# Two-layer hybrid encoder on one core: another order between layer 0's mixer and its experts, row turns ahead of the third modulation tile, and q products that take hT chunk by chunk

## The chip, the core and the metric

One core of one Trainium2 chip runs the whole kernel in one launch. Five engines matter: TensorE (PE in the rows, PEld its weight loads), VectorE (DVE), ScalarE (ACT), GpSimd (POOL) and SyncE (SP), which only issues DMAs here. Each takes its instructions in the order in which they are written and waits at semaphores; nothing is scheduled by a compiler. The metric is the device time of one execution in microseconds, 942.29 for the kernel before (median of three).

## The reference, cut to what matters

256 tokens of width 1024 go through two layers, all in float32. The part that the change touches:

```
mod = silu(c) @ ada_w[layer] + ada_b[layer]            # six rows of 1024: shift, scale, gate, twice
h = rmsnorm(x) * norm_mix_g * (1 + scale) + shift
z = h @ w_in                                           # q 512, k and v 256, xr 512, gate 512
m = concat([window_attention(q, k, v), rg_lru(xr) * gelu(gate)]) @ w_out      # layer 0's mixer
x = x + g_m * m
h = rmsnorm(x) * norm_ffn_g * (1 + scale_f) + shift_f
group = argmax(h @ wg + bg); two best of the group's 4 experts by h @ we + be
x = x + g_f * sum over experts of gate_e * (silu(h @ w1[e]) * (h @ w3[e])) @ w2[e]
```

Layer 1 has an S5 state-space mixer in place of attention and LRU (`y = C h + d u`, with complex tables made from `s5_b`, `s5_c` and the poles), a GLU, and again 16 experts in 4 groups. A final norm ends the kernel.

## The kernel before, in words

All state lives in SBUF. `x` is [128, 2, 1024]: two blocks of 128 tokens. `hT` is the normalised, modulated input turned to features by tokens, in 8 chunks of 128 features; TensorE turns `xhat` (`turn_x`), ScalarE writes chunks 0, 1, 4, 5 and VectorE 2, 3, 6, 7 (`modulate`, semaphores `hT_act` and `hT_dve`). Weights come in tiles of 2 MB: `ring` has six slots, and one more place, `aslot` in `work`, serves the modulation weights. SyncE issues these DMAs in one fixed order; before each it waits until the last reader of the slot has signalled.

**Front.** The first four modulation tiles (`ada(0, 4)`: eight products each, condition column by weights into one row of `bank[7]`) give layer 0's first shift and scale. TensorE turns small parameter rows to columns (`tr` of `rows` and `brow`, ScalarE copies them at L635 and L636), ScalarE copies the modulation row (`rows_out`, L642), `ada_cols` makes columns of it, VectorE adds the bias, and then both engines modulate. The q products (L1429) wait for all of `hT`. GpSimd issues small loads beside this, among them four for the LRU's block-diagonal gate weights (`gaw`), which are used at about 102 us.

**Mixer's exit.** The output product has four tiles (`mix_out`, L1563), token block b by column half h, each in two halves of the inner dimension: attention's first, LRU's second. Between the second halves stand `ada_cols(1)` (twelve more modulation rows to columns, L1387) and `gate_row(0)` (L1412), which spreads the gate g_m over all partitions; ScalarE copies it to `grow` (L629, L630). VectorE's `residual` then multiplies and adds tile by tile (L1109, L1110) and signals `x_new`.

**Tables of layer 1.** S5's C matrices are loaded to `Cn` by four DMAs that ScalarE issues after the LRU (L725). TensorE turns them, four groups of four blocks (`turn_tables(0, 4)`, L1352), ScalarE writes the result to `H1` (`table_evac(0, 4)`, eight instructions, L742). GpSimd makes the B tables G0 and G1 from `Bl` in 16 products (L507 to L511), then `over_row(0)`, which finds whether a group has more tokens than slots, and then 16 pieces of rotation table, each written to DRAM.

**Experts.** `ffn(L)` norms, turns and modulates x, makes the router's logits (L1665, L1670), and VectorE picks group and experts in a chain of small instructions up to `member_ready`. TensorE ranks the tokens by products with a triangle of ones (L1682 to L1686, `rank_ps`), VectorE makes the group's one-hot picks (L1189, `pick_ready`). `open_acc(m)` starts one of four accumulators in banks 4 to 7 with a product that gives zeros (L1676). A loop over the four groups then gathers tokens (L1633), turns the weighted picks (`weights`, which waits for VectorE's L1197), and runs up, gate and down products of each expert (L1606 or L1609, L1625) and the scatter (L1649). Layer 0's groups run the narrow form, 64 slots. Twelve 2 MB tiles are loaded per group; a slot's next DMA waits for the product that last read it.

What sets the order: the text of each engine's function alone.

## Time and profile before

| | |
|---|---|
| time, median of 3 | 942.29 us (941.72 to 944.27) |
| the profiled execution | 942.3 us, its span 940.5 us |
| TensorE, VectorE, ScalarE, GpSimd busy | 842.9, 294.2, 191.1, 168.4 us |
| TensorE's clock, mean of what was granted | 0.952 |
| DMA | 285.32 MB, 303 GB/s over the span |
| chain of waits by engine | TensorE 80%, DMA 8%, VectorE 5%, ScalarE 3% |

The profile is one execution. A timeline row gives start and duration from the span's start, engine, line of the kernel, operation, tiles, how many instructions are merged in it, and in brackets the idle time before it and what ended it. A float32 product appears as two MATMUL records. "issue" is time in which an engine waited for nothing that the profile shows.

### The profile page before, as it was taken

Reading aid. Unit: us, or ns where it says so; the run is one execution under the profiler, and the core shown is the slowest. Engines: PE = TensorE matmul, PEld = TensorE weight load, DVE = VectorE, ACT = ScalarE, POOL = GpSimd, SP = SyncE. Lnnn points to the kernel's source line nnn. Section 1 sums busy time; section 2 is a strip of 40 time slices with the busy share of each in tenths; the row PEclk is TensorE's granted clock in tenths of the full one; section 3 lists DMA queues with packets and bytes.
Section 4 is the critical chain, followed back from the end, with each engine's and each line's share of the span. In section 5 each row is a group of like instructions: output and inputs, shape, how many; then the busy total and the mean of one; then the engine's idle time right before and its main releaser. Section 6 shows DMA issues by size and latency. Waiting matters only on the chain.

```text
span 940.5 us, 12765 instructions
## 1 busy us (share of the span) xinstructions
PE 842.9 (90%) x5229; PEld 460.6 (49%) x5230; DVE 294.2 (31%) x694; ACT 191.1 (20%) x310; POOL 168.4 (18%) x258
## 2 busy tenths in 40 slices
PE   2699999799999998999599998799998899999992
PEld 0367644565455463553456543444443554654641
DVE  1347432641131320311799411530000310412214
ACT  1313330421221311311500101320001212213111
POOL 3201009186343434400033100100000000000000
PEclk9799999689999999999889999699999899999997
DMA  9999999539999999996996882208775399999961
GB/s 307 345 382 284 343 384 357 192 108 400 393 400 402 391 400 401 391 393 250 388 376 232 325 293 101 80 5 297 289 255 194 103 398 391 397 397 392 392 241 69
DMA packets 126288, 285.32 MB, mean 303 GB/s; under 512 B 7092, under 2 KB 8388, under 8 KB 125992
## 3 DMA queue, kind: packets, MB, share of 16 engines
q1 hardware_dynamic: 119392, 276.83, 80.0%
q0 software_dynamic: 1984, 5.21, 2.0%
q10 hardware_dynamic: 4872, 2.72, 1.0%
q8 instruction: 29, 0.48, 0.2%
q14 instruction: 11, 0.09, 0.0%
HBM read 279.50 MB, written 5.24 MB: 303 GB/s over the span
## 4 chain that ended last, share of the span: by engine, by line
PE 80%; DMA 8%; DVE 5%; ACT 3%; SPq 2%; issue 2%; ACTq 1%; DVEq 0%
PE PS L1606 19%; PE PS L1625 13%; PE PS L1633 8%; PE PS L1649 7%; PE PS L1894 6%; PE PS L1609 6%; PE PS L1377 4%; PE PS L1352 4%; PE PS L1446 3%; DMA yg<-in_s_c_im 3%; DMA ring<-in_moe_w 2%; DMA work<-in_ada_w 2%; PE PS L1429 2%; PE PS L1879 2%; SPq L340 1%
## 5 line engine op out<-in xcount | busy, mean ns | idle before, releaser
L1625 PE MATMUL PS<-ring,work 128*64 128x512 f32 (+1 forms) x512 | 130.5, 597 | 6.2 <-ACT work L779 6.2
L1606 PE MATMUL PS<-ring,hT 128*64 128x256 f32 x896 | 109.0, 385 | 3.0 <-DMA ring<-in_moe_w 3.0
L1606 PE MATMUL PS<-ring,yg 128*64 128x256 f32 x896 | 106.6, 379 | 0.0
L1606 PEld LDWEIGHTS PS<-ring,hT 128*64 128x64 f32 x896 | 66.8, 138 | 40.9 <-issue 9.3
L1625 PEld LDWEIGHTS PS<-ring,work 128*64 128x64 f32 (+1 forms) x512 | 43.1, 143 | 85.5 <-issue 85.5
L1218 DVE TENSOR_TENSOR work<-work,PS 128x512 f32<-128x512 f32 x32 | 22.0, 688 | 195.0 <-PE PS L1606 147.2
L1633 PE MATMUL PS<-work,xhat 128*128 128x256 f32 (+1 forms) x256 | 76.3, 451 | 7.0 <-issue 7.0
L1606 PEld LDWEIGHTS PS<-ring,yg 128*64 128x64 f32 x896 | 67.6, 137 | 29.2 <-issue 0.2
L1222 DVE COPY yg<-PS 128x512 f32<-128x512 f32 x32 | 22.1, 691 | 180.5 <-PE PS L1625 180.5
L1649 PE MATMUL PS<-yg,grow 64*128 64x512 f32 (+1 forms) x256 | 70.1, 612 | 7.1 <-DVE yg L1222 7.1
L1633 PEld LDWEIGHTS PS<-work,xhat 128*128 128x128 f32 x256 | 48.7, 205 | 38.8 <-issue 21.7
L1894 PE MATMUL PS<-ring,yg 128*128 128x512 f32 x128 | 58.6, 603 | 0.0
L1377 PE MATMUL PS<-ring,condz 128*32 128x512 f32 x320 | 42.5, 659 | 12.8 <-DMA ring<-in_ada_w 12.7
L783 ACT ACTIVATE yg<-PS 128x512 f32<-128x512 f32 x32 | 19.1, 597 | 166.5 <-PE PS L1625 166.5
L1649 PEld LDWEIGHTS PS<-yg,grow 64*128 64x128 f32 (+1 forms) x256 | 25.7, 186 | 35.9 <-issue 22.1
L775 ACT ACTIVATE work<-PS 128x512 f32<-128x512 f32 x32 | 19.1, 597 | 104.9 <-PE PS L1606 79.6
L1894 PEld LDWEIGHTS PS<-ring,yg 128*128 128x128 f32 x128 | 23.2, 190 | 33.6 <-issue 33.6
L779 ACT ACTIVATE work<-PS 128x512 f32<-128x512 f32 x32 | 19.1, 597 | 96.7 <-PE PS L1352 96.7
L1352 PE MATMUL PS<-ident,work 128*128 128x128 f32 x176 | 28.7, 284 | 6.7 <-ACT yg L783 6.3
L1352 PEld LDWEIGHTS PS<-ident,work 128*128 128x128 f32 x176 | 18.9, 141 | 26.7 <-issue 25.9
L552 POOL TENSOR_TENSOR work<-work 128x512 f32<-128x512 f32 x16 | 16.7, 1046 | 80.4 <-DMA rot_tables<-work 80.3
L1207 DVE TENSOR_SCALAR hT<-PS,modA,mod 128x512 f32<-128x512 f32 x16 | 13.0, 810 | 57.5 <-PE PS L1633 57.5
(351 smaller groups left out, 966.9 us busy)
## 6 DMA issues: line engine op xcount, KB each, us to landing
ring<-in_moe_w SPq DMA_DIRECT2D x96, 2048.0 KB, 16.8
ring<-in_ada_w SPq DMA_DIRECT2D x20, 2048.0 KB, 14.9
work<-in_ada_w SPq DMA_DIRECT2D x4, 2048.0 KB, 13.9
ring<-in_s_glu_w SPq DMA_DIRECT2D x4, 2048.0 KB, 16.0
ring<-in_ab_w_in SPq DMA_DIRECT2D x3, 2048.0 KB, 21.3
ring<-in_ab_w_out SPq DMA_DIRECT2D x2, 2048.0 KB, 13.6
rot_tables<-work POOLq DMA_DIRECT2D x16, 256.0 KB, 5.8
ring<-rot_tables SPq DMA_DIRECT2D x2, 2048.0 KB, 10.7
```

The source lines that it names most:

```text
L775: s.activation(he[:, e % 2, :], bank[0], ACT.Silu).then_inc(S("sil_ready"), 1)
L1218: v.tensor_tensor(he[:, e % 2, :], he[:, e % 2, :], bank[1], ALU.mult).then_inc(S("he_ready"), 1)
L1222: v.tensor_copy(yg[:, e % 2, HALF:], bank[3]).then_inc(S("y_dve"), 1)
L1352: return nc.tensor.transpose(dst, src, ident[0:n, 0:n])
L1377: last = mm(bank[7][32 * j:32 * j + 32, :], condz[:, k, 32 - r:64 - r], ada_unit(u)[:, k, :], start=any(first) and k < 4, stop=any(final) ...
L1446: last = mm(dst, w[:, k, :], hT[:, k, :], start=k == 0, stop=k == KD - 1)
L1606: last = mm(dst[64 * u:64 * u + 64, 0:256], hg[k][:, e * P:e * P + 64], w[:, k, 256 * u:256 * u + 256], start=k == 0, stop=k == KD - 1)
L1609: last = mm(dst, hg[k][:, e * P:(e + 1) * P], w[:, k, :], start=k == 0, stop=k == KD - 1)
L1625: last = mm(dst, heT[:, at:at + (64 if narrow else P)], w[:, c4, h * HALF:(h + 1) * HALF], start=c4 == 0, stop=c4 == KF - 1)
L1633: last = mm(bank[k % 2].rearrange("p (e n) -> p e n", n=P)[:, :, 0:n_s], xhat[:, b, k * P:(k + 1) * P], pick[:, b, :, 0:n_s], start=b == 0 ...
L1649: last = mm(acc[2 * b + h], pickT[pp, e, b * P:(b + 1) * P], yg[pp, at, h * HALF:(h + 1) * HALF], start=False, stop=False)
L1894: last = mm(bank[GLU_BANK[m][part]], actT[:, k, b * P:(b + 1) * P], u3(n)[:, k, :], start=False, stop=k == KD - 1)
```

## The change

Seven edits, in the order of the program:

- the four `gaw` loads on GpSimd come after its wait for the fourth modulation tile
- TensorE turns `rows` and `brow` ahead of the third modulation tile; the q products of the first token block wait for hT chunk by chunk
- the four `Cn` loads are issued by SyncE, after the last early modulation tile and ahead of the first expert tiles
- `ada_cols(1)` stands after the first output tile and `gate_row(0)` after the second, each one tile earlier
- layer 0's `turn_tables(0, 4)` and `table_evac(0, 4)` move from before the norm into the routing; the four groups use other banks, and one accumulator (bank 5) is opened last, after their copies
- ScalarE copies the second gate row before the router's exponentials, in both layers; layer 1 opens three accumulators before the rank products and one behind them
- GpSimd runs `over_row(0)` before the B tables

```diff
-        TABLES = ((2, 0, 0, 6), (2, 0, 1, 7), (2, 1, 0, 4), (2, 1, 1, 5),
+        TABLES = ((2, 0, 0, 0), (2, 0, 1, 5), (2, 1, 0, 2), (2, 1, 1, 3),
@@ SyncE
+            sp_.wait_ge(S("pv_done"), 6)
+            for v, name in enumerate(("s5_c_re", "s5_c_im")):
+                for u in range(2):
+                    sp_.dma_start(Cn[:, v, :, u * 64:(u + 1) * 64],
+                                  a[name][0].rearrange("(k g) c p -> (g c) k p", k=KD)).then_inc(S("cn_in"), 16)
@@ GpSimd
+            pool.wait_ge(S("ada_used"), ADA_FIRST)
             for v, name in enumerate(("ab_gate_a_w", "ab_gate_x_w")):
...
-            pool.wait_ge(S("ada_used"), ADA_FIRST)
...
+            over_row(0)
             for tab, c0 in ((G1, 3), (G0, 5)):
...
-            over_row(0)
@@ ScalarE
-            for v, name in enumerate(("s5_c_re", "s5_c_im")):
-                for u in range(2):
-                    s.dma_start(Cn[:, v, :, u * 64:(u + 1) * 64],
-                                a[name][0].rearrange("(k g) c p -> (g c) k p", k=KD)).then_inc(S("cn_in"), 16)
...
-                if L == 0:
-                    table_evac(0, 4)
-                else:
+                if L == 1:
                     s.activation(warm, ones[:, 0:1], ACT.Sqrt)
                 norm(n)
                 modulate(n)
+                gate_row(n)
...
-                gate_row(n)
                 act.wait_ge(S("l2_ready"), L + 1)
                 s.activation(exp_2, mx2, ACT.Exp).then_inc(S("exp_ready"), 1)
+                if L == 0:
+                    table_evac(0, 4)
@@ TensorE
             turn_x(0)
-            ada(2, ADA_FIRST)
             pe.wait_ge(S("rows_in"), 16 * (len(ROWS) + 2))
...
+            ada(2, ADA_FIRST)
             ada_cols(0)
-            hT_ready(0)
...
+                    if b == 0:
+                        pe.wait_ge(S(("hT_act", "hT_dve")[k // 2 % 2]), k // 4 * 2 + k % 2 + 1)
...
+                if (b, h) == (0, 0):
+                    ada_cols(1)
                 if (b, h) == (0, 1):
-                    ada_cols(1)
-                if (b, h) == (1, 0):
                     gate_row(0)
...
-            turn_tables(0, 4)
             pe.wait_ge(S("x_new"), 1)
...
-                open_acc(0)
-                open_acc(1)
+                for m in (0,) if L == 0 else (0, 1, 2):
+                    open_acc(m)
+                if L == 0:
+                    turn_tables(0, 4)
                 pe.wait_ge(S("member_ready"), L + 1)
...
-                open_acc(2)
-                open_acc(3)
+                for m in (2, 3) if L == 0 else (3,):
+                    open_acc(m)
+                if L == 0:
+                    pe.wait_ge(S("tab_evac"), 4)
+                    open_acc(1)
                 pe.wait_ge(S("narrow_known"), L + 1)
```

TensorE from the second halves of the mixer's output (L1563) to the first turn of layer 0's x (L1352 with `xhat`); L1387 is `ada_cols`, L1412 `gate_row`, L1352 with `yg` the C table. Before:

```order
L1563 MATMUL PS<-ring,yg 128x512 x7
L1387 MATMUL PS<-sel,work 128x12 [waits ada_rows]
L1387 MATMUL PS<-sel,work 128x12 x3
L1563 MATMUL PS<-ring,yg 128x512 x4
L1412 MATMUL PS<-ident,mod 128x128 [waits mod_cols]
L1412 MATMUL PS<-ident,mod 128x128 x7
L1563 MATMUL PS<-ring,yg 128x512 x4
L1352 MATMUL PS<-ident,yg 128x128 [waits cn_in]
L1352 MATMUL PS<-ident,yg 128x128 x7
L1352 MATMUL PS<-ident,yg 128x128 [waits grow_ready]
L1352 MATMUL PS<-ident,yg 128x128 x7
L1352 MATMUL PS<-ident,xhat 128x128 [waits xhat_ready,x_new]
```

The same place now, each line of the text one lower:

```order
L1563 MATMUL PS<-ring,yg 128x512 x3
L1386 MATMUL PS<-sel,work 128x12 [waits ada_rows]
L1386 MATMUL PS<-sel,work 128x12 x3
L1563 MATMUL PS<-ring,yg 128x512 x4
L1411 MATMUL PS<-ident,mod 128x128 [waits mod_cols]
L1411 MATMUL PS<-ident,mod 128x128 x7
L1563 MATMUL PS<-ring,yg 128x512 x8
L1351 MATMUL PS<-ident,xhat 128x128 [waits xhat_ready,x_new]
```

Columns and gate row moved up by one tile, so two tiles stand behind the gate row, and the C table's 16 turns with their two waits left this place.

TensorE in layer 0's routing, from the router's second product (L1670) to the branch into the groups; L1676 opens accumulators, L1682 to L1686 are the rank products. Before:

```order
L1670 MATMUL PS<-sel,work 128x20 [waits strips_out]
L1670 MATMUL PS<-sel,work 128x20
L1676 MATMUL PS<-condz,before 128x512 x2
L1682 MATMUL PS<-rt,before 128x16 [waits member_ready]
L1683 MATMUL PS<-rt,before 128x16
L1684 MATMUL PS<-rt,ones 128x16
L1686 MATMUL PS<-rt,ones 128x16 x2
L1676 MATMUL PS<-condz,before 128x512 x2
L1692 UNCONDITIONAL_BRANCH [waits narrow_known]
```

And now (L1674 opens):

```order
L1674 MATMUL PS<-condz,before 128x512
L1351 MATMUL PS<-ident,yg 128x128 [waits cn_in]
L1351 MATMUL PS<-ident,yg 128x128 x7
L1351 MATMUL PS<-ident,yg 128x128 [waits grow_ready]
L1351 MATMUL PS<-ident,yg 128x128 x7
L1682 MATMUL PS<-rt,before 128x16 [waits member_ready]
L1683 MATMUL PS<-rt,before 128x16
L1684 MATMUL PS<-rt,ones 128x16
L1686 MATMUL PS<-rt,ones 128x16 x2
L1674 MATMUL PS<-condz,before 128x512 x2
L1674 MATMUL PS<-condz,before 128x512 [waits tab_evac]
L1695 UNCONDITIONAL_BRANCH [waits narrow_known]
```

The 16 turns stand between one opening and the rank products, and three openings stand behind the rank products where two stood, the last with a wait for ScalarE's table copies.

GpSimd after its memsets, before (L507 to L511 the B tables, L488 the start of `over_row`):

```order
L475 MEMSET work 128x2048
L507 TENSOR_TENSOR work<-work,s5c 128x512 [waits s5c_ready,ada_used,bl_in,pool_order]
L508 TENSOR_TENSOR work<-work,s5c 128x512
L511 TENSOR_TENSOR work<-work 64x32x16 [waits pool_order] x2
L507 TENSOR_TENSOR work<-work,s5c 128x512 [waits pool_order]
```

And now:

```order
L479 MEMSET work 128x2048
L492 TENSOR_SCALAR rt<-rt 128x4 [waits ada_used,s5c_ready,narrow_known,bl_in,pool_order]
L493 TENSOR_SCALAR rt<-rt 128x4
L494 TENSOR_SCALAR rt<-rt 128x32
L495 TENSOR_TENSOR rt<-rt 128x4 [waits pool_order]
```

The table products follow 15 instructions of the overflow row, whose first waits for `narrow_known`, the end of the routing.

## Rows read from the trace of the kernel before

**Rows 1.** Chain of waits, 120 to 200 us: start us, us, what.
```profile
141.64 23.93 DMA yg<-in_s_c_im
172.26 3.65 PE PS L1352 x16
```

**Rows 2.** Timeline of TensorE, 20 to 60 us: start, us, then as above.
```profile
31.25 3.64 PE L1377 MATMUL PS<-work,condz 128*32 128x512 f32 x16 [3.50 <-DMA work<-in_ada_w]
...
36.68 1.87 PE L1387 MATMUL PS<-sel,work 128*128 128x4 f32 x8 [1.09 <-ACT work L642]
41.07 15.40 PE L1429 MATMUL PS<-ring,hT 128*128 128x512 f32 x32 [2.52 <-ACT hT L623]
```

**Rows 3.** Timeline of ScalarE, 30 to 60 us.
```profile
36.03 0.59 ACT L642 ACTIVATE work<-PS 128x512 f32<-128x512 f32 x1
...
39.07 1.93 ACT L623 ACTIVATE hT<-PS,mod,modA 128x256 f32<-128x256 f32 x4 [0.93 <-DVE modA L930]
```

**Rows 4.** DMA queues, 7 to 17 us: packets, MB, share of 16 engines.
```profile
q0 software_dynamic: 256, 0.30, 22.7%
```

**Rows 5.** Timeline of TensorE, 143 to 200 us.
```profile
157.24 1.95 PE L1412 MATMUL PS<-ident,mod 128*128 128x128 f32 x16
159.03 3.60 PE L1563 MATMUL PS<-ring,yg 128*128 128x512 f32 x8
...
185.49 3.78 PE L1676 MATMUL PS<-condz,before 1*128 1x512 f32 x4
189.20 10.21 PE L1633 MATMUL PS<-work,xhat 128*128 128x256 f32 x32
```

**Rows 6.** Timeline of ScalarE, 143 to 200 us.
```profile
148.19 0.60 ACT L642 ACTIVATE work<-PS 128x512 f32<-128x512 f32 x1 [13.83 <-issue]
...
166.30 3.14 ACT L742 ACTIVATE work<-PS 64x256 f32<-64x256 f32 x8 [5.99 <-PE PS L1352]
169.47 1.06 ACT L613 ACTIVATE xhat<-x 128x1024 f32<-128x1024 f32 x1
```

**Rows 7.** Timeline of VectorE, 139 to 200 us.
```profile
160.40 0.69 DVE L1109 TENSOR_TENSOR xhat<-PS,grow 128x512 f32<-128x512 f32 x1 [5.70 <-ACT grow L630]
...
166.12 1.05 DVE L1110 TENSOR_TENSOR x<-x,xhat 128x512 f32<-128x512 f32 x1
...
186.81 1.66 DVE L1189 TENSOR_SCALAR work<-slotv,rt 128x128 f32<-128x128 f32 x8
```

**Rows 8.** Timeline of all engines, 585 to 660 us, layer 1's routing.
```profile
587.26 0.69 DVE L1335 TENSOR_TENSOR x<-x,work 128x512 f32<-128x512 f32 x1
...
604.32 3.78 PE L1676 MATMUL PS<-condz,before 1*128 1x512 f32 x4
...
610.28 15.80 PE L1633 MATMUL PS<-work,xhat 128*128 128x512 f32 x32 [2.18 <-issue]
```

**Rows 9.** Two stretches: us, busy us of PE, PEld, DVE, ACT, POOL, clock, DMA.
```profile
146.20:166.70 20.50, 17.51 (x66) 9.51 (x66) 6.89 (x11) 2.07 (x5) 19.53 (x16) 1.00 1.08 365
183.90:194.00 10.10, 10.10 (x24) 6.58 (x24) 5.01 (x25) 0.78 (x1) 6.34 (x31) 0.50 0.00 0
```

**Rows 10.** Timeline of VectorE in groups 0 and 2 of layer 0.
```profile
200.18 2.54 DVE L1197 TENSOR_SCALAR work<-slotv,rt 128x128 f32<-128x128 f32 x8
...
326.37 4.04 DVE L1197 TENSOR_SCALAR work<-slotv,rt 128x128 f32<-128x128 f32 x8
...
331.07 1.66 DVE L1189 TENSOR_SCALAR work<-slotv,rt 128x128 f32<-128x128 f32 x8
```

**Rows 11.** Timeline of TensorE in the same groups.
```profile
206.40 1.09 PE L1352 MATMUL PS<-ident,work 128*128 128x128 f32 x8
...
364.99 0.69 PE L1606 MATMUL PS<-ring,hT 128*64 128x256 f32 x2 [2.29 <-DMA ring<-in_moe_w]
```

**Rows 12.** DMA queues, 203 to 440 us: packets, MB, share of 16 engines.
```profile
q1 hardware_dynamic: 36000, 88.08, 98.0%
q0 software_dynamic: 1280, 4.20, 4.4%
```

More of the change, by code:

```diff
@@ L1586, in turn_tables @@
                     if n_ == 2:
-                        pe.wait_ge(S("grow_ready"), 1)
+                        pe.wait_ge(S("grow_ready"), 2)
                     if n_ == 7:
```

1 line of the change is left out of this document (removed).

## The prediction

> **What bounds the kernel now.** I read the shares by engine first: TensorE works for nine tenths of the span, so every edit is priced by what it does to TensorE's idle time. Then I read the chain of waits from 120 to 200 us, the only long stretch where another resource leads. It runs through one table load: the C table of the S5 layer is sent from ScalarE's queue at 141.64 and lands 23.93 us later, at 165.57 [rows 1]. TensorE turns that table before it turns x, and x is turned only at 172.26 [rows 1]. Then come the front of the kernel on TensorE and ScalarE [rows 2, 3], the mixer's exit and the routing on TensorE, ScalarE and VectorE [rows 5 to 7], and last the DMA account of layer 0's experts [rows 11, 12], which says whether a gain ahead of them survives them.
>
> **Front.** Three edits. (a) The four gate-weight DMAs leave the first 17 us. GpSimd's queue moved 0.30 MB there, 22.7% of ten microseconds of all 16 engines, 2.3 us, and nearly all of it was these weights [rows 4]. TensorE then waits for the fourth modulation tile, which arrives at 31.25 [rows 2]. By bytes, 0.30 MB at the kernel's 397 MB per ms (88.08 + 4.20 MB in the 233 us of the experts' stream [rows 12]) is 0.8 us; by engine time it is 2.3. I take 1.2 us, ends 0.6 and 2.0. (b) The row turns stand ahead of the third tile, so ScalarE's two small copies are done early and the copy of the modulation rows can start when the last modulation product ends, at 34.89, instead of at 36.03 [rows 2, 3]: 1.1 us. It asks that the rows have landed when the second tile is through; ScalarE issues them before anything else it does. (c) The q products start on the first hT chunk. They start now at 41.07; the chunks start at 39.07, four in 1.93 us on ScalarE [rows 2, 3], so the first is there at 39.55: 1.5 us. A q product is two passes of 15.40/32 = 0.48 us [rows 2], as long as two chunks, so TensorE doesn't starve. Sum 3.8 us, from 2.2 to 4.6. From 41 to 146 TensorE has hardly an idle microsecond and VectorE and ScalarE follow it, so I let all of it through.
>
> **Mixer's exit, in the clock times of before.** TensorE does the same products in another order, so the last output tile ends at 162.63 as before [rows 5]. The gate row's products stood in front of that one tile and ended at 159.03, where it starts; now two tiles of 3.6 us stand behind them, so they end at 155.5, 3.5 us earlier. What they need is earlier too: the copy of the modulation rows waited at 148.19 for ScalarE's DMA issues, 13.83 us of "issue" [rows 6], which are gone. ScalarE's copy of the gate row follows in 1.3 us, at 156.8. The residual adds started at 160.40 and ended with the add at 166.12, 1.05 us long [rows 7]; now three of the four pairs run before the last tile, and the fourth waits for it at 162.65. Each add was lengthened while GpSimd built tables; the same add with GpSimd idle takes 0.69 [rows 8], and GpSimd's tables have moved away. x is new at 162.65 + 0.69 + 0.72 = 164.1 instead of 167.2: 3.1 us. Then ScalarE's eight table copies (3.14 us from 166.30) stood in front of its square at 169.47 [rows 6]; they are gone from there. From the square to the first turn of x is 172.26 - 169.47 = 2.8 us [rows 1, 6], so x is turned at 166.9. **Gain 5.4 us.** The table's turns are hidden in TensorE's wait for VectorE's routing, and what covered the C table's flight is no longer needed: it is issued some ten microseconds earlier (SyncE sends it when attention is done) and wanted some six later.
>
> **Routing.** What is late next is TensorE's own queue. Before, two of the four openings of accumulators stood after the rank products, 3.78 us, and the gather began when they ended, at 189.20, though VectorE's picks were done at 188.47 [rows 5, 7]. Now three stand there. The granted clock is 0.5 in that stretch [rows 9], the 1.2 GHz level, and an opening costs 1.89. **Loss 1.9 us**; if the turned tables keep the clock at 2.4 GHz (an opening about 1.0, and a gather about 2 us shorter) it is a gain of some 2. I take the low clock, since it fell before while TensorE was occupied with such short products. ScalarE's table copies (3.14 us) end before the second opening does. In layer 1 the move goes the other way: three openings ahead, one behind; 1.9 us less from 604.32, minus 0.25 because the third may push the rank products. The gather came 2.18 us after the last opening with nothing to wait for [rows 8]. **Gain 1.6 us**, ends 0 and 2.
>
> **Layer 0's experts.** From the release of the first slot (203) to the last landing (about 440) the DMA engines are full: 98.0% for weights and 4.4% for the rotation tables [rows 12], and TensorE has to wait for weights for any length once, 2.29 us at 364.99 [rows 11]. So this stage ends when its bytes have come. The stream starts at the first release, and before it the DMA share is 0.00 [rows 9]: it can start as much earlier as TensorE does, and the whole shift goes through. GpSimd's table products (19.53 us busy in the 20.5 us up to 166.70 [rows 9]) now come behind the overflow row, so the rotation writes fall 20 us later against the experts, but all 4.20 MB still lie inside the stream: no change at its end.
>
> They have a second effect. Picks and weights of the first group (16 short VectorE instructions) now run beside those products. While GpSimd made three such products, eight weight instructions took 4.04 us; the eight picks behind them, undisturbed, took 1.66 [rows 10]. They were done at 202.72 [rows 10], and TensorE wants them at 206.40 [rows 11], 3.7 us later. By that row eight instructions take 2.4 us more, and at most about 5 if the overlap is twice as long: a wait of 0 to 1.5 us.
>
> The Trainium skill, page "SBUF — State Buffer", section "Who interferes with whom", has GpSimd and VectorE's two-port instructions lock each other out for a whole instruction. With one of 16 table products (19.53/16 = 1.2 us) ahead of each weight, TensorE would wait about 3.6 us. The 4.04 us row agrees in kind.
>
> Either way the DMA stream hides it, since its first two releases come before. What I book for this stage is 0.3 us of loss for a second dip of the clock at a wait on weights (a dip costs 1.7 us).
>
> **Sum.** 3.8 + 5.4 - 1.9 + 1.6 - 0.3 = 8.6 us. The profiled execution took 942.3 (span 940.5, 1.8 around it), the same as the median 942.29, so it needs no scaling: **933.7 us**.
>
> **Rivals.** 1. *The clock stays up through the routing.* Table turns fill the gap in which it fell. For it: 2.6 us of full-width turns. Against: in layer 1's routing too the stretch after the rank products is slow (3.78 us for two openings). Then 933.7 - 3.9 = 929.8.
> 2. *The experts take part of it back.* The first group stalls for the weights by the skill's 3.6 us or more, long enough to delay the slots, or TensorE meets the DMA stream twice with the clock down: 2 to 4 us, 936.7. For it: the 4.04 us row. Against: the stream is full anyway.
> 3. *The front is bound by arrivals.* The fourth tile comes no earlier and the layer-1 opening is hidden behind the picks: 933.7 + 1.2 + 1.6 = 936.5.
> 4. *The other side: the C table comes late.* On the sync queue its four small-packet DMAs stand behind four modulation tiles (8.4 MB, 21 us) and in front of six expert tiles. TensorE is in order: behind the table's first turn wait the rank products, three openings and the gather. It is wanted at about 172 - 3.8 = 168; each microsecond past that costs one, and past 177 the kernel is slower than before. Landing behind all expert tiles, at about 183, gives 933.7 + 15 = 949. For it: they took 23.93 us once [rows 1]. Against: they now stand first in line, and should land near 150.
>
> The skill's page "DMA: Bandwidth & Descriptors", section "Issuing engines are not separate DMA queues", says that the engine which issues changes only the issue time; by it the move to the sync queue makes the transfer itself no faster, and only its place in line counts.
>
> 5. *The change doesn't do what it says* (x turned no earlier, for a wait that I missed in the new order): 939.
>
> **How the numbers follow.** Forecast 0.50, rival 1 0.14, rivals 2 and 3 together 0.26, rival 4 0.03, rival 5 0.07. My own case spans 931.5 to 936. To leave out no more than 2 in 10 the range takes in rivals 1 to 3: 929.5 to 938.0. This measurement can tell 0.3%, 2.8 us, from no change, so faster means under 939.5: 0.92; same 0.05; slower 0.03.
>
> **What would show it.** q products starting near 37.3; the gate row's copy done near 153.3 and x turned near 163; no ScalarE DMA issue at 134; table turns on TensorE between the first opening and the rank products, without a wait for a DMA; three openings behind them, 5.6 us at 1.2 GHz; gather near 182; layer 0's last weight landing 7 us earlier; layer 1's gather 1.6 us sooner after its rank products. A gather later than 185, or an expert stage longer than 260 us, would prove me wrong.

## The result: 934.85 us, predicted 933.7, with three terms wrong that nearly cancel

| | before | after |
|---|---|---|
| time, median (range) of the runs set side by side | 942.0 us (941.72 to 944.27), 4 runs | 934.85 us (932.28 to 935.47), 4 runs |
| ratio | | 0.9914, 95% interval 0.9889 to 0.9938 |
| the profiled execution, its span | 942.3, 940.5 us | 934.65, 932.8 us |
| TensorE's clock, mean | 0.952 | 0.961 |

The kernel became 7.2 us faster by the medians (8.1 by the means, from which the ratio is made), inside the range of 929.5 to 938.0. In what follows the two profiled executions are set against each other, 7.65 us apart.

### The profile after

The page of the kernel after, parts 1 and 4. TensorE is busy 5.2 us less than before, and in the chain VectorE has gone from 5% to 8% while DMA has gone from 8% to 2%: one kind of wait has gone and another has come.

```profile
PE 837.7 (90%) x5229; PEld 458.6 (49%) x5230; DVE 308.2 (33%) x694; ACT 191.3 (21%) x310; POOL 167.3 (18%) x258
...
PE 85%; DVE 8%; DMA 2%; issue 2%; ACT 2%; SPq 1%; DVEq 0%; ACTq 0%
```

Chain of waits of the kernel after, 120 to 205 us (start us, us, what). The 23.93 us of the C table's load [rows 1] are nowhere in it. VectorE's weights (L1196, L1197 before) are new in it.

```profile
162.67 2.99 PE PS L1351 x16
...
176.57 1.73 DVE work L1188 x8
178.30 0.24 issue
178.54 6.32 PE PS L1632 x16
...
189.69 9.59 DVE work L1196 x8
199.33 1.09 PE PS L1351 x8
```

Timeline of TensorE after, 18 to 60 us (start, us, engine, line, operation, tiles, count, idle before and what ended it), to be read beside [rows 2].

```profile
29.39 2.84 PE L1376 MATMUL PS<-work,condz 128*32 128x512 f32 x16 [3.49 <-DMA work<-in_ada_w]
32.93 1.87 PE L1386 MATMUL PS<-sel,work 128*128 128x4 f32 x8 [0.70 <-ACT work L645]
36.03 16.19 PE L1429 MATMUL PS<-ring,hT 128*128 128x512 f32 x32 [1.23 <-ACT hT L626]
```

The fourth modulation tile is 1.86 us earlier. The idle time ahead of the columns is 0.70 instead of 1.09, the one ahead of the q products 1.23 instead of 2.52. They start 5.04 us earlier. They also take 0.79 us longer, so that the rest of the mixer runs 4.24 us ahead.

Timeline of TensorE after, 143 to 202 us, beside [rows 5].

```profile
149.56 1.95 PE L1411 MATMUL PS<-ident,mod 128*128 128x128 f32 x16
151.34 7.03 PE L1563 MATMUL PS<-ring,yg 128*128 128x512 f32 x16
162.67 2.99 PE L1351 MATMUL PS<-ident,xhat 128*128 128x128 f32 x16 [4.29 <-DVE xhat L905]
...
170.74 1.97 PE L1351 MATMUL PS<-ident,yg 128*128 128x128 f32 x16
173.30 0.40 PE L1682 MATMUL PS<-rt,before 128*128 128x16 f32 x2 [0.59 <-DVE rt L1151]
...
174.52 3.04 PE L1674 MATMUL PS<-condz,before 1*128 1x512 f32 x6
178.54 10.39 PE L1632 MATMUL PS<-work,xhat 128*128 128x256 f32 x32 [0.98 <-DVE work L1188]
...
199.33 1.09 PE L1351 MATMUL PS<-ident,work 128*128 128x128 f32 x8 [3.34 <-DVE work L1196]
```

The 16 turns of the C table (L1351 with `yg`) wait for nothing. Three openings take 3.04 us, and the gather waits 0.98 us for VectorE's picks instead of following the openings. Then TensorE stands idle 3.34 us at 199 for the weighted picks; before, it had them in time [rows 11].

Four stretches of the kernel after (us, busy us of PE, PEld, DVE, ACT, POOL, clock, DMA). The granted clock falls to 0.5 only at about 177 us. GpSimd is busy 6.43 of the seven microseconds from 177 to 184, and from 179.9 on with the table products; before, it had only the overflow row and other short instructions there (31 of them, 6.34 us [rows 9]).

```profile
168.00:174.00 6.00, 5.41 (x42) 4.38 (x40) 3.52 (x20) 4.46 (x10) 0.00 (x0) 1.00 0.93 345
174.00:177.00 3.00, 3.00 (x12) 1.52 (x11) 2.62 (x15) 2.42 (x4) 0.42 (x2) 1.00 0.04 16
177.00:184.00 7.00, 6.02 (x14) 4.37 (x14) 2.18 (x9) 0.78 (x1) 6.43 (x18) 0.51 0.00 1
```

Timeline of VectorE after, group 0's weights; they took 2.54 us before [rows 10].

```profile
189.69 9.58 DVE L1196 TENSOR_SCALAR work<-slotv,rt 128x128 f32<-128x128 f32 x8
```

Timeline of GpSimd after, from the same moment.

```profile
189.57 1.06 POOL L512 TENSOR_TENSOR work<-work,s5c 128x512 f32<-128x512 f32 x1
190.59 1.06 POOL L513 TENSOR_TENSOR work<-work,s5c 128x512 f32<-128x512 f32 x1
191.73 2.63 POOL L516 TENSOR_TENSOR work<-work 64x512 f32<-64x512 f32 x2
```

Eight VectorE instructions took as long as eight of GpSimd's: each got in once per table product. GpSimd's own were not lengthened (1.06 and 1.3 us apiece, as elsewhere). The same happened in group 3, where GpSimd's H0 products (L566 to L571) started at 381.48 and met the weights. Timeline of TensorE after, 385 to 395 us:

```profile
391.98 1.93 PE L1351 MATMUL PS<-ident,work 128*128 128x128 f32 x8 [3.29 <-DVE work L1196]
```

And of GpSimd after, 381 to 393 us:

```profile
381.48 1.04 POOL L566 TENSOR_TENSOR work<-work,s5c 128x512 f32<-128x512 f32 x1 [5.18 <-DMA rot_tables<-work]
```

Timeline of TensorE after in layer 1's routing, beside [rows 8]: one opening stands behind the rank products, and the gather comes hardly sooner.

```profile
597.30 2.07 PE L1674 MATMUL PS<-condz,before 1*128 1x512 f32 x2
603.13 1.19 PE L1632 MATMUL PS<-work,xhat 128*128 128x512 f32 x1 [3.76 <-issue]
```

### Where the 7.65 us come from

Each line is how far the kernel after has come ahead at that point, from starts of the same instructions in the two traces. These are two executions; which parts hold in the others is said behind the experiments.

| point | before | after | ahead | this part |
|---|---|---|---|---|
| second halves of the mixer's output | 145.94 | 141.70 | 4.24 | +4.2 front |
| x turned | 172.26 | 162.67 | 9.59 | +5.4 mixer's exit |
| layer 0's first gather | 189.20 | 178.54 | 10.66 | +1.1 routing |
| group 1's gather | 254.41 | 247.33 | 7.08 | -3.6 group 0 |
| group 2's gather | 317.50 | 310.43 | 7.07 | 0 |
| group 3's gather | 385.60 | 373.53 | 12.07 | +5.0 group 2 |
| layer 1's first turn of x | 458.10 | 451.00 | 7.10 | -5.0 group 3 |
| layer 1's first gather | 610.28 | 603.13 | 7.15 | +0.1 its routing |
| end of the profiled execution | 942.3 | 934.65 | 7.65 | +0.5 |

### The profile page after: what moved, and what is told of

The parts are those of the page before. It is cut to its first block, busy times and chain, and to the rows that moved or that the text cites. A ratio compares the mean times of both kernels' runs of the same rounds, so it can differ in the third digit from the quotient of the medians.

```text
span 932.8 us, 12766 instructions
## 1 busy us (share of the span) xinstructions
PE 837.7 (90%) x5229; PEld 458.6 (49%) x5230; DVE 308.2 (33%) x694; ACT 191.3 (21%) x310; POOL 167.3 (18%) x258
## 4 chain that ended last, share of the span: by engine, by line
PE 85%; DVE 8%; DMA 2%; issue 2%; ACT 2%; SPq 1%; DVEq 0%; ACTq 0%
PE PS L1605 20%; PE PS L1624 14%; PE PS L1632 8%; PE PS L1648 7%; PE PS L1897 6%; PE PS L1608 6%; PE PS L1376 4%; PE PS L1351 4%; PE PS L1446 3%; PE PS L1563 3%; DMA work<-in_ada_w 2%; DVE work L1196 2%; PE PS L1429 2%; PE PS L1882 2%; PE PS L1860 1%
## 5 line engine op out<-in xcount | busy, mean ns | idle before, releaser
L1217 DVE TENSOR_TENSOR work<-work,PS 128x512 f32<-128x512 f32 x32 | 22.0, 687 | 183.8 <-PE PS L1605 136.1
L1605 PEld LDWEIGHTS PS<-ring,yg 128*64 128x64 f32 x896 | 67.5, 137 | 29.1
L1376 PE MATMUL PS<-ring,condz 128*32 128x512 f32 x320 | 41.3, 641 | 11.7 <-DMA ring<-in_ada_w 11.7
L1351 PE MATMUL PS<-ident,work 128*128 128x128 f32 x176 | 29.5, 290 | 13.3 <-DVE work L1196 6.6
L1351 PEld LDWEIGHTS PS<-ident,work 128*128 128x128 f32 x176 | 19.6, 144 | 33.5 <-issue 25.2
L1196 DVE TENSOR_SCALAR work<-slotv,rt 128x128 f32<-128x128 f32 x64 | 34.6, 613 | 0.0
## 6 DMA issues: line engine op xcount, KB each, us to landing
ring<-in_moe_w SPq DMA_DIRECT2D x96, 2048.0 KB, 15.9
ring<-in_s_glu_w SPq DMA_DIRECT2D x4, 2048.0 KB, 16.3
```

Source lines behind the costliest of these rows:

```text
L1196: last = v.tensor_scalar(pickW[:, b, e, :], slotv, k9[:, b * EPG + e:b * EPG + e + 1], gt[:, b, e:e + 1], ALU.is_equal, ALU.mult)
L1351: return nc.tensor.transpose(dst, src, ident[0:n, 0:n])
L1376: last = mm(bank[7][32 * j:32 * j + 32, :], condz[:, k, 32 - r:64 - r], ada_unit(u)[:, k, :], start=any(first) and k < 4, stop=any(final) ...
L1605: last = mm(dst[64 * u:64 * u + 64, 0:256], hg[k][:, e * P:e * P + 64], w[:, k, 256 * u:256 * u + 256], start=k == 0, stop=k == KD - 1)
```

## Experiments

Eleven experiments ran, one of them (E10) the kernel after once more. Those of one group share a chip and the runs of the kernel before, 943.8, 944.5 and 943.3 us in median, somewhat above the 942.0 of the first comparison; so ratios are compared, and parts of the kernel in the traces.

### Experiments 1 to 4: GpSimd's tables, and the front alone

E1, the order of GpSimd undone:

```diff
-            over_row(0)
             for tab, c0 in ((G1, 3), (G0, 5)):
...
             pool.sem_inc(S("b_tables"), 1)
+            over_row(0)
```

> The kernel after, with GpSimd's B tables ahead of the overflow row again, as in the kernel before; all else as after. Theory: in layer 0's first group TensorE waits 3.3 us for the weighted picks because GpSimd's 16 table products run beside VectorE's eight weight instructions (9.6 us instead of 2.5). With the tables about 142 to 162 us the eight take 2.5 us again, that wait is gone, and group 1's gather starts about 10 us earlier than in the kernel before instead of 7.1; in group 3 GpSimd's H0 products end before the weights, so the second such wait (3.3 us) goes too, but the waits for weight tiles in group 2 (3.0 us) come back. The residual adds cost 0.6 us more beside the tables. Sum about 932.3 us (931 to 933.5). Rival, as the prediction has it: the DMA stream sets the end of the stage and hides the wait for picks; then only the 0.6 us show, about 935.4, and TensorE waits for weight tiles for what it saved.

Measured: 933.12 us (932.04 to 936.8, 6 runs), ratio 0.9897 (0.9876 to 0.9918), inside the theory's range. Group 1's gather comes 9.0 us earlier than before (245.38 against 254.41).

E2, tables late:

```diff
             over_row(0)
+            pool.wait_ge(S("weight_ready"), 1)
             for tab, c0 in ((G1, 3), (G0, 5)):
```

> The kernel after, with one wait more: GpSimd makes the B tables only when group 0's weighted picks are done. Theory (VectorE and GpSimd hold each other up): neither the residual adds nor the weights of group 0 meet table products, and the H0 products move about 12 us later, behind group 3's weights. 3.3 us of wait in group 0 and 3.3 us with a clock drop (1.7) in group 3 are gone; against it up to 4.7 us of waits for weight tiles in group 2 come back, as in the kernel before. 934.85 - 8.3 = 926.5 at best, 931.2 at worst, 929 taken. Rival: the DMA stream sets the end of the stage; then about 934.9, with waits for weight tiles in place of the picks.

Measured: 930.15 us (928.8 to 932.37, 4 runs), ratio 0.9864 (0.9841 to 0.9887), inside the range.

E3, split:

```diff
-            over_row(0)
             for tab, c0 in ((G1, 3), (G0, 5)):
+                if tab is G0:
+                    over_row(0)
...
             pool.wait_ge(S("tab_evac"), 4)
+            pool.wait_ge(S("weight_ready"), 4)
```

> The kernel after, with half of the B tables (G1) made ahead of the overflow row, in the time in which GpSimd idles before the residual adds, the other half (G0) behind it, where it should end at about 189.6 as group 0's weights begin; and the H0 products wait until group 3's weighted picks are done. Theory: as with late tables, 929 us (926.5 to 931.2), and within 1 us of the kernel with late tables, since in both no table product meets the picks. If it is slower than that one by 2 us or more, G0's tail meets the weights or the rotation writes, 10 us earlier, take DMA time that TensorE wants. Rival (the DMA stream sets the end): 934.9.

Measured: 932.25 us (931.72 to 933.17, 4 runs), ratio 0.9881 (0.986 to 0.9903). That is above the range, and 2.1 us above E2 by the medians, though the two intervals overlap. G0's tables didn't meet the weights, which took 2.24 us; TensorE waits for a tile in group 2 instead, as the table below shows.

E4, the front's three edits on the kernel before, as in the diff of the change:

> The kernel before with the three edits of the front alone (gate-weight loads behind the fourth modulation tile, row turns ahead of the third tile, q products chunk by chunk). The traces of before and after stand 4.2 us apart from 56 to 141 us. Theory: these 4.2 us come through whole, 937.8 us (937.2 to 938.5), since the layer-0 stream starts as much earlier as TensorE does. The prediction's own term: 3.8, 938.2. Rival: the stream of layer 0's weights gives part or all of it back, 939.5 to 942.

Measured: 938.01 us (936.34 to 939.98, 6 runs), ratio 0.9942 (0.9924 to 0.9961). The front is worth 0.58% (0.39 to 0.76), 5.5 us against that day's 943.78; in the trace it is 5.0 us ahead at the turn of x ahead of layer 0's experts (167.27 against 172.26) and 4.8 at the end of layer 0's experts (453.31 against 458.10). It comes through. That a part of its gain varies with the clock is told below.

The timeline of VectorE in E1, group 0's weights:

```profile
191.15 2.64 DVE L1196 TENSOR_SCALAR work<-slotv,rt 128x128 f32<-128x128 f32 x8
```

And in E2, from the weights to the picks:

```profile
188.68 2.13 DVE L1197 TENSOR_SCALAR work<-slotv,rt 128x128 f32<-128x128 f32 x8
190.98 1.01 DVE L1230 COPY rt<-rt 128x9 f32 x1 [0.17 <-DVE work L1197]
192.02 1.00 DVE L1183 TENSOR_SCALAR slotv<-slot_no,rt 128x64 f32<-128x64 f32 x1
193.06 6.39 DVE L1189 TENSOR_SCALAR work<-slotv,rt 128x128 f32<-128x128 f32 x8
```

With the tables out of the way the eight weights take 2.64 and 2.13 us, and TensorE turns them without a wait. In E2 the tables start right behind them, and now the picks take 6.39 us instead of 1.66. TensorE wants those one group later, so it costs 0.59 us only, at VectorE's next product. From the first gather to the second, group 0 takes 65.3 us in E1 and 65.6 in E2, against 65.2 before, 68.8 after and 67.4 in E10, the kernel after once more. That the table products made the wait is shown.

E1 also shows what their old place costs. VectorE in E1 at the mixer's exit:

```profile
157.88 0.98 DVE L1109 TENSOR_TENSOR x<-x,xhat 128x512 f32<-128x512 f32 x1
158.90 2.18 DVE L898 CUSTOM_DVE_ANT_0 xhat<-x 128x1024 f32<-128x1024 f32 x1
161.01 0.08 DVE L898 DVE_READ_ACCUMULATOR2_ANT stat<- 128x1 f32 x1
161.12 1.10 DVE L901 TENSOR_SCALAR stat<-stat 128x2 f32<-128x2 f32 x1
```

The sum of squares takes 2.18 instead of 1.22 us, and an instruction of two numbers per partition takes 1.10 instead of 0.17. From x being new to its turn 4.7 us pass instead of 2.8. So the new order on GpSimd moved a loss of 2.2 us from the exit (0.3 of it the add) to 3.6 us in group 0. Between these two traces it was a bad trade by 1.4 us. Against E10, where group 0 takes only 2.2 us more than before, it was an even one, and the times of E1 and the kernel after don't tell them apart (0.9897 against 0.9914 and 0.9903). Making the tables after the weights avoids both losses.

Where the rest of the gain in E1 to E3 went is seen in groups 2 and 3, from gather to gather, and to the turn of x, us:

| kernel | group 0 | group 2 | group 3 | 2 and 3 | TensorE waits there for |
|---|---|---|---|---|---|
| before | 65.2 | 68.1 | 72.5 | 140.6 | tiles, 0.71 and 2.29 |
| after | 68.8 | 63.1 | 77.5 | 140.6 | weighted picks, 3.29 |
| E1 tables first | 65.3 | 67.9 | 72.5 | 140.4 | tiles, 0.35 and 2.30 |
| E2 tables late | 65.6 | 63.1 | 76.2 | 139.3 | tiles, 1.01 and 1.75 |
| E3 split | 65.7 | 67.5 | 73.5 | 141.1 | tiles, 2.31 |

Two stalls take turns. Where the H0 products meet group 3's weights, TensorE falls back by 3.3 us and the tiles are there in time. Where they don't, it catches up with the stream of weight tiles and waits for it. The sum is the same within 2 us. My theory had counted both, 8.3 us at best, and E2 got 3.2 in group 0 and 1.3 here (68.8 to 65.6, and 140.6 to 139.3).

### Experiments 5 to 8: the form of the instruction, the C table's place, the openings, the gate loads

E5:

```diff
-                            last = v.tensor_scalar(pickW[:, b, e, :], slotv, k9[...],
-                                                   gt[:, b, e:e + 1], ALU.is_equal, ALU.mult)
+                            last = v.scalar_tensor_tensor(pickW[:, b, e, :], slotv, k9[...],
+                                                          gt[:, b, e:e + 1].to_broadcast([P, P]), ALU.is_equal, ALU.mult)
```

> The kernel after, with VectorE's eight weight instructions of each group in another form: one operation with the slot numbers and the group weight as two full input tensors (SCALAR_TENSOR_TENSOR) in place of TENSOR_SCALAR with two scalars. GpSimd's B tables stay beside them. Theory A (the two engines lock each other out for whole instructions only when VectorE's instruction is of the fast form, which took 0.34 us undisturbed and 1.08 to 1.43 beside the tables): the new form takes longer undisturbed, perhaps 0.4 us, but is lengthened little, as the residual adds of the kernel before were (0.69 to 1.05): eight take 3.5 to 4.5 us, TensorE doesn't wait at 199, and the time is about 931. Theory B (any pair of VectorE and GpSimd on SBUF takes turns, each VectorE instruction waits for a GpSimd instruction of 1.05 to 1.3 us whatever its form): still 9 to 10 us and a wait of 3 us or more, 934.9.

Measured: 934.67 us (933.99 to 937.08, 6 runs), ratio 0.9902 (0.9886 to 0.9918). VectorE in E5:

```profile
188.43 8.71 DVE L1196 SCALAR_TENSOR_TENSOR work<-slotv,rt 128x128 f32<-128x128 f32 x8
```

TensorE waits 2.48 us at 197 and 3.18 in group 3. Theory A falls: this form is held up as much. Undisturbed, in group 2, the eight take 2.18 us, and the old form in E10, whose wait is nearly the same (2.44), takes 8.67. Theory B in its width falls too, since not every VectorE instruction is held up: the products of the residual, which read one operand from PSUM, took 0.68 or 0.69 us in E1 beside the tables as in the kernel after without them, while the adds on SBUF took 0.83 to 1.05 there and 0.69 here. The Trainium skill, page "SBUF — State Buffer", section "Who interferes with whom", says both: an instruction with two SBUF inputs contends with a GpSimd instruction that reads SBUF, and one with at most one SBUF input, outside the two-port modes, does not. These traces agree. How much is lost differs, though: the 128x512 adds were lengthened by 0.14 to 0.36 us, and not by a whole GpSimd instruction.

E6, the C table's turns and copies ahead of the norm again, two openings ahead of the rank products in layer 0 (banks, waits and openings follow the kernel before and are left out of this excerpt):

```diff
 # ScalarE, ffn(L)
+                if L == 0:
+                    table_evac(0, 4)
...
-                if L == 0:
-                    table_evac(0, 4)
 # TensorE
+            turn_tables(0, 4)
             pe.wait_ge(S("x_new"), 1)
...
-                if L == 0:
-                    turn_tables(0, 4)
```

> The kernel after, with the C table's 16 turns and ScalarE's eight copies of them back ahead of the norm, where the kernel before has them, and two openings ahead of the rank products in layer 0; loads, gate row, front and GpSimd as after. Theory: the turns fit into TensorE's wait for x (158.3 to 162.7, 3.3 us of turns), but the copies, 3.1 us, stand in front of ScalarE's square, so x is turned 1.5 to 3 us later, at about 164.2 to 165.7; and the routing has a gap of TensorE again in which the clock falls, as in the kernel before, so that the openings behind the rank products take 3.8 us and the gather starts cold: gather at 182 to 185 instead of 178.5. Group 0's wait for the weighted picks shrinks by as much as the gather comes later, since GpSimd's tables start at the same point of the routing: no, they start with the routing's end and so move too; 3.3 us stay. Sum 937 to 940. Rival: the clock in the routing doesn't depend on the turns; then only the exit's 1.5 to 3 us show, 936.4 to 938, with openings of 0.43 us behind the rank products.

Measured: 938.61 us (935.57 to 942.56, 6 runs), ratio 0.9944 (0.9922 to 0.9967). TensorE in E6, where the gap ahead of the rank products is back:

```profile
175.75 0.40 PE L1682 MATMUL PS<-rt,before 128*128 128x16 f32 x2 [1.63 <-DVE rt L1151]
...
177.54 3.78 PE L1676 MATMUL PS<-condz,before 1*128 1x512 f32 x4
181.25 1.22 PE L1633 MATMUL PS<-work,xhat 128*128 128x256 f32 x2
```

Against E10 below, the kernel after in an execution with the same front (second halves of the mixer's output at 141.17 and 141.15), x is turned 2.17 us later (164.30 against 162.13), and the gather starts 2.79 us later (181.25 against 178.46). By the ratios E6 is 2.8 to 3.9 us slower than the kernel after (0.9914 and 0.9903), where the theory had 2 to 5. The theory had the place right, and the time. It overrated the routing, gather at 182 to 185, which costs 0.6 us and not several: VectorE's picks end at 178.2 in E10, so the gather could hardly have come sooner, however short the openings.

E7, layer 1's openings two and two; E8, the gate loads alone on the kernel before:

```diff
-                for m in (0,) if L == 0 else (0, 1, 2):
+                for m in (0,) if L == 0 else (0, 1):
...
-                for m in (2, 3) if L == 0 else (3,):
+                for m in (2, 3):
```

> The kernel after, with layer 1's openings two ahead of the rank products and two behind, as in the kernel before. Theory: in layer 1 the gather's start hangs on narrow_known and on the code of the wide form, which one instruction load of 0.02 MB brings in 1.9 us behind it; the gather follows narrow_known by 4.8 to 5.0 us whatever the openings do. The openings end at about 601.1 in that case and the gather starts 5.8 to 6.0 us after the first opening behind the rank products, as in both traces so far: no change (0 to 0.15 us). Rival (the prediction's): the gather comes a fixed 2.2 us behind the last opening, 1.6 us later than in the kernel after.

> The kernel before with one of the front's three edits, the four gate-weight loads behind GpSimd's wait for the fourth modulation tile. Theory: the third and the fourth tile land 1.86 us sooner (25.79 to 23.93 and 31.21 to 29.35 between the traces of before and after), the modulation products, their copy and the q products follow by that: q products start at 39.2 instead of 41.07. Prediction's term: 1.2 us, 39.9. Rival: the arrival of the tiles doesn't hang on these loads and varies from run to run; then the q products start at 41.

One profiled execution each, 936.19 and 941.62 us. Timeline of TensorE in E7, layer 1's routing:

```profile
598.82 3.78 PE L1674 MATMUL PS<-condz,before 1*128 1x512 f32 x4
604.83 2.04 PE L1632 MATMUL PS<-work,xhat 128*128 128x512 f32 x2 [2.23 <-issue]
```

Timeline of TensorE in E8, the fourth modulation tile and the first q products:

```profile
30.11 3.51 PE L1376 MATMUL PS<-work,condz 128*32 128x512 f32 x16 [3.33 <-DMA work<-in_ada_w]
...
38.75 2.06 PE L1428 MATMUL PS<-ring,hT 128*128 128x512 f32 x2 [2.52 <-ACT hT L622]
```

In E7 the gather starts 6.01 us behind the first opening after the rank products, in the kernel after 5.83 with one opening fewer there, before 5.96. The opening isn't what it waits for: the theory holds, on one trace of each kernel. That it is the code of the wide form is a likely reading and no more: one instruction load of 0.02 MB stands 1.9 us behind `narrow_known` in both traces, and layer 0, which runs the narrow form, starts its gather 0.24 us behind the picks with no load of that queue in between. No run here took that load away.

In E8 the gate loads alone bring the fourth tile 1.14 us forward, 31.25 to 30.11, near the prediction's term and not the 1.86 of the theory. The two differ mostly by where the first tile landed: from the first modulation product (13.76 before, 13.34 after, 13.97 in E8) to the fourth tile's it takes 17.49 us before, 16.05 after and 16.14 in E8. So the loads are worth about 1.4 us. The q products start 2.3 us sooner, below both forecasts: 1.14 of it is the tile, 0.4 its products and the row turns, and 0.8 the columns, which ran at the full clock here (1.05 us for 1.87). The q products themselves then take 1.0 us longer (16.38 for 15.40), and 1.3 us are left behind them (54.96 against 56.30). In the eleven traces whose front was changed in full the fourth tile's products start between 29.39 and 30.11. The rates fit: from 12 to 17 us the DMA engines moved 288 GB/s before, 377 in E8 and 381 after, all with a full busy share.

### Experiments 9 to 11: what the late tables leave

E9, on E2, the rotation table's writes sent before the stream:

```diff
             over_row(0)
+            ch.link(g.memset(stage, 0.0))
+            for k in range(KD):
+                for v in range(2):
+                    pool.dma_start(rot_d[:, k, v, :], stage).then_inc(S("rot_out"), 16)
             pool.wait_ge(S("weight_ready"), 1)
+            pool.wait_ge(S("rot_out"), 32 * KD)
...
+            pool.wait_ge(S("weight_ready"), 2)
             for k in range(KD):
...
-                    pool.dma_start(rot_d[:, k, v, :], stage).then_inc(S("rot_out"), 16)
...
+            pool.wait_ge(S("weight_ready"), 3)
```

> The kernel with late tables, but the 16 writes of the rotation table to DRAM (4.2 MB) are sent in one go right behind the overflow row, at about 180 to 190 us, when no other DMA is under way, from a zeroed tile; the table that layer 1 reads is zero, so its result isn't the reference's. The products of the table are still made, after group 1's weights (the rotation pieces) and after group 2's (H0), so that they meet no weights. Theory: what TensorE waits for in group 3 of the kernel with late tables (1.0 and 1.8 us for weight tiles) is the DMA time that the rotation writes take from the weight stream, 4.2 MB at 385 GB/s, 11 us; without them in the stream these waits go and the time is 927.3 (926 to 928.5). Rival: the weight stream alone is too slow for TensorE; the waits stay, 930.

Measured: 928.26 us (927.02 to 929.04, 5 runs), ratio 0.9834 (0.9819 to 0.985). Groups 2 and 3 take 63.1 and 73.0 us, together 136.1 instead of 139.3, and TensorE waits for no weight tile at all. Its one wait, 0.42 us in group 1, is for a VectorE product, behind picks of 6.16 us that met GpSimd's tables. So E2's waits for tiles come from the DMA time of the rotation writes. That is shown for E2, whose waits (0.17, 1.01 and 1.75) are nearly all of the 3.2 us gained; for the waits of the other kernels it is likely and not tested. E9 moves GpSimd's products too, but they move no bytes. E2 reads, in the timeline of TensorE in group 3,

```profile
412.17 1.95 PE L1606 MATMUL PS<-ring,hT 128*64 128x256 f32 x16 [1.01 <-DMA ring<-in_moe_w]
...
417.59 1.95 PE L1606 MATMUL PS<-ring,hT 128*64 128x256 f32 x16 [1.75 <-DMA ring<-in_moe_w]
```

And E9's timeline of TensorE at the same place reads

```profile
412.69 1.90 PE L1610 MATMUL PS<-ring,hT 128*64 128x256 f32 x16
...
416.14 1.90 PE L1610 MATMUL PS<-ring,hT 128*64 128x256 f32 x16
```

E10, the kernel after once more:

> The kernel after itself, once more, on the same chip and beside the same runs of the kernel before as the two others, so that they can be set against each other. Expected 934.5 to 936 where the kernel before takes 943 to 944.5, a ratio of 0.9914 as first measured. In its trace the two waits of 3.3 us for the weighted picks should stand again, in groups 0 and 3. If the fourth modulation tile's products run at the full clock in this execution (1.9 us instead of 2.8), everything behind them is 0.9 us earlier.

Measured: 934.09 us (932.97 to 935.68, 5 runs), just below the range, ratio 0.9903 (0.9885 to 0.992). The two waits for weighted picks stand again, but with 2.44 and 2.32 us instead of 3.34 and 3.29, since the eight weights take 8.67 us and not 9.58. TensorE waits 1.12 us for a tile in group 2: the two stalls share the time here. The three openings take 3.97 us instead of 3.04. Timeline of TensorE in E10, group 0:

```profile
197.87 1.09 PE L1351 MATMUL PS<-ident,work 128*128 128x128 f32 x8 [2.44 <-DVE work L1196]
```

E11, G1's tables ahead of the overflow row, G0's after group 0's weights, H0 after group 3's:

> Late tables improved: G1's half of the B tables is made ahead of the overflow row, in GpSimd's idle time from 141 us, G0's half after group 0's weighted picks, and the H0 products after group 3's. Theory: the same two waits gone as with late tables; the rotation writes end about 10 us earlier than there, so that they lie under group 2 rather than group 3. Whether TensorE waits less for weight tiles isn't clear from the traces: late tables left 2.8 us of waits in group 3, the split without the wait 2.3 us and a clock drop in group 2. 928 to 932, 930 taken. Rival: G1's products, 142 to 151 us, meet the first residual adds and x comes later, 930.5 or more.

Measured: 930.78 us (929.71 to 932.64, 5 runs), ratio 0.987 (0.9852 to 0.9887). Waits for tiles are 0.53 us in group 2 and 0.86 and 1.73 in group 3. It is no better than E2: the rotation writes lie elsewhere in the stream, and their bytes are the same.

The kernel with late tables (E2), one line more than the kernel after, is the fastest of those that leave nothing out: 0.9864 against 0.9903 for the kernel after, intervals 0.9841 to 0.9887 and 0.9885 to 0.992, which just touch. The two weren't timed beside each other. E11 (0.987) and E3 (0.9881) can't be told from E2.

## Why the prediction was right, point by point

The number was right in part by luck. The front and the mixer's exit went as forecast. Behind them the case that was given 0.50 didn't happen: the clock stayed up for a while, as in rival 1, the first group stalled for its weights, as in rival 2, and layer 1's opening gave nothing, as in rival 3. These three departures nearly cancel.

**Front, 3.8 predicted, 4.2 measured.** (a) The gate loads: 1.2 predicted, 1.14 alone in E8, 1.86 in the profiled execution of after, 1.4 when counted from the first tile. (b) Row turns: 1.1 predicted, 1.09 measured (from the end of the modulation products to the columns 1.79 before, 0.70 after). The copy of the modulation rows now stands right behind the last modulation product, at 32.28. (c) Chunk by chunk: 1.5 predicted, 1.29 measured (idle 2.52 to 1.23). Where the modulation products ran at the full clock (E1, E2, E3, E5) the q products wait for their own weights instead, 1.71 us at 35, which is this front's next limit. What the sum left out is the clock: TensorE's products of the fourth tile took 0.8 us less, the q products 0.8 more. With it the front's gain moves: the second halves of the mixer's output start 2.8 (E7) to 6.0 us (E5) ahead of the one trace of before in the eleven traces with this front, 4.8 in E10. That 4.2 came so near 3.8 is luck in that measure.

**Mixer's exit, 5.4 predicted, 5.35 measured.** The gate row's copy ended at 152.6, x was new at 159.8 and turned at 162.67, near 163. The steps are as predicted, with all four adds at 0.69 us. This part is firm: from the second halves to x turned it takes 26.32 us before and 20.97 to 20.99 in all eight traces with the whole exit changed. E1 shows that 2.2 us of the 5.35 hang on GpSimd being idle there, and E6 that another 2.2 hang on ScalarE's table copies being gone.

**Routing, a loss of 1.9 predicted, a gain of 1.1 measured: wrong.** The step that failed is "I take the low clock". The turned tables kept it for a while: the granted clock was 1.00 up to 177 us, as rival 1 had it, and three openings took 3.04 instead of 5.6 us. Rival 1 was too rosy as well. It wanted 3.9 us more than the forecast and 3.0 came, since the gather then waits for VectorE's picks and is cold as before (10.39 against 10.21 us). E6, with the gap back, has two openings of 3.78 us back. The gain of 1.1 isn't firm either. From x's turn to the first gather it takes 16.9 to 17.0 us in the four traces without the turns in the routing (before, E4, E6, E8). In the nine with them it takes 15.8 to 17.3: 15.9 after, 16.3 in E10, and 16.9 to 17.3 in E2, E3 and E5, where the clock falls within the openings (three take 4.43 to 4.92 us) and nothing is gained.

**Layer 0's group 0, a wait of 0 to 1.5 us predicted and hidden, 3.6 us measured and not hidden: wrong twice.** The size: I priced eight held-up instructions by a row in which only part of them had met GpSimd, 4.04 us, where the pace is one VectorE instruction per GpSimd instruction, 9.58 us. By the rule of the Trainium skill (page "SBUF — State Buffer", section "Who interferes with whom"), cited beside it, the wait came out at 3.6 us, an estimate. The traces decide for it, with 3.34 us after, 3.05 and 3.12 in E6 and E7, and 2.44 in E10. The cover: "its first two releases come before" was true, and they came 10.5 us earlier (192.74 against 203.22). But every later release of a slot hangs on TensorE, which stood still; the third came at 204.22 instead of 211.30, 7.1 us earlier. A stream whose slots the waiting engine frees doesn't hide that engine's wait.

**The stream lets the shift through: right.** At group 1's gather and again at layer 1 the kernel after is 7.1 us ahead, and E1 9.0 and 9.3. A loss of 0.3 for a second dip of the clock was predicted, 0 measured here; in E5 the dip came behind group 0's wait (the first up products 3.49 us instead of 1.95), and group 0 took 69.1 us. Below it two stalls of some 5 us changed places, which the prediction didn't see: against TensorE, the H0 products moved by 20 us (from 11.7 ahead of group 3's gather to 8.0 behind it), onto group 3's weights.

**Layer 1's openings, 1.6 us predicted, 0.1 measured: wrong.** "The gather came 2.18 us after the last opening with nothing to wait for" is a wait for something that the profile doesn't name. I read a fixed distance where there was a fixed time from the rank products; E7 shows it.

**C table on the sync queue (rival 4):** landed by 140.5, wanted at 170.7. The move cost nothing.

Sum by measured terms: 4.2 + 5.4 + 1.1 - 3.6 + 0.1 + 0.5 = 7.7 us, against 8.6. The forecast landed within 1.2 us because the routing was too dark by 3.0 and group 0 and layer 1 too bright by 3.3 and 1.5; 0.4 of the front and 0.5 behind layer 1's gather, which no term had, make up the rest. Of the sentences on what would prove it wrong none came true (gather at 178.5; from the first slot's release to the end of group 3 it took 255.5 us, 252.1 before). Of those on what would show it right, the q products (36.0 against 37.3), the gate row, x, the table's turns and the missing ScalarE issues did; the openings, the gather at 182, the last landing (9.4 us earlier, 439.5 to 430.1, not 7) and layer 1's gather did not.

## What to carry to other kernels

When work moves on GpSimd, list what VectorE does on SBUF beside its new place, and price each short TENSOR_SCALAR, COPY or SCALAR_TENSOR_TENSOR there, however small, at one whole GpSimd instruction (the long adds lost 0.14 to 0.36 us, the products with an operand in PSUM nothing); then ask whether another engine waits for them within that time. A wait of "issue" at a fixed distance behind an instruction is no proof that the instruction sets it: measure the distance from other events in a second place before selling the instruction. A full DMA stream hides a stall only if its slots are freed by somebody other than the stalled engine. And where the clock of a sparse stretch differs from run to run, one pair of traces doesn't settle a term of a microsecond: compare the stretch in every trace there is.

## What the runs showed of the hardware beyond the question

- Beside GpSimd's products of 1.05 to 1.3 us, VectorE instructions of very different size took nearly the same time: 128x2 1.10, 128x9 1.01, 128x64 1.00, 128x128 1.02 to 1.44 us. GpSimd's were mostly untouched; beside VectorE's long sum of squares two of GpSimd's took 3.81 instead of 2.61 us.
- The first products run at either clock from one execution to the next, with the same front (granted clock 1.00 in E1 and 0.50 in E9 from 30.0 to 31.5 us). The fourth modulation tile's 16 products took 1.92 us in E1, E2, E3 and E5, 2.84 in the kernel after, and 3.3 to 3.64 in E4, E6, E7 and E9 to E11, with the same front in all of them and with nearly equal arrivals (29.4 to 30.1). The kernel after alone had 2.84 and, as E10, 3.42. The spread is 1.7 us, beside the 3 us by which runs of one kernel differ here.
- The clock's fall at the gather isn't avoided by filling the gap in front of it, only put off. With the table's turns in the routing it fell at 177 us in the kernel after, and already within the openings in E2, E3, E5, E10 and E11 (their last records take 1.06 us each instead of 0.59). The gather took 9.8 to 10.7 us in each, where the later groups' take 8.1.
